# Fourier stage of a two-layer trunk: half the channel columns, time folded a second time, mirrored channels joined in the output weights

## The reference, cut to what matters

```python
def fourier_mix(u, w_f):
    B, T, _ = u.shape
    ug = u.astype(F32).reshape(B, T, FNET_GROUPS, FNET_GROUP_DIM)
    f = jnp.fft.fftn(ug, axes=(1, 3), norm="ortho").real.astype(u.dtype).reshape(B, T, FNET_WIDTH)
    return f @ w_f
```

## Time and profile before

| | |
|---|---|
| median of 3 runs | 2941.22 us (2939.51 to 2941.58) |
| span of the profiled execution | 2938.6 us |
| busy: TensorE, its weight loads | 2877.4 us, 2756.4 us |
| busy: VectorE, ScalarE, GpSimd | 1330.6, 1076.5, 614.0 us |
| instructions | 44082, of which 18396 matmul passes |
| granted clock of TensorE | 0.996 of full speed over the span |

### The profile page before, as it was taken

How to read it: one execution, slowest core, us unless ns; L and a number is a source line. 1 busy time by engine, 2 the same in 40 slices (tenths; PEclk the granted TensorE clock), 3 DMA queues, 4 the chain that set the end, 5 groups by cost and what they waited for, 6 DMA issues and landing times.

```text
span 2938.6 us, 44082 instructions
## 1 busy us (share of the span) xinstructions
PE 2877.4 (98%) x18396; PEld 2756.4 (94%) x18396; DVE 1330.6 (45%) x2291; ACT 1076.5 (37%) x1947; POOL 614.0 (21%) x312
## 2 busy tenths in 40 slices
PE   6999999999999999999999999999999999999998
PEld 5999999999999999999999999999999989899997
DVE  4343443123557575446344434421146567554543
ACT  4333333221444544422343333323133444443231
POOL 0221221122221212122431221211221121211242
PEclk9999999999999999999999999999999999999999
DMA  5332224102111102254421121220211111215532
GB/s 224 102 110 82 102 90 137 67 15 78 42 47 47 48 32 94 80 203 141 133 79 65 66 82 39 94 83 22 70 41 45 44 48 47 78 51 183 165 110 94
DMA packets 84278, 248.55 MB, mean 85 GB/s; under 512 B 9201, under 2 KB 30193, under 8 KB 83057
## 3 DMA queue, kind: packets, MB, share of 16 engines
q1 hardware_dynamic: 84080, 245.74, 24.5%
HBM read 191.71 MB, written 54.00 MB: 84 GB/s over the span
## 4 chain that ended last, share of the span: by engine, by line
PE 89%; DVE 5%; ACT 2%; DMA 2%; issue 1%; SPq 1%; DVEq 0%; POOL 0%; POOLq 0%; ACTq 0%
PE ps L730 44%; PE ps L713 18%; PE ps L823 6%; PE ps L769 6%; PE ps L900 3%; PE ps L1041 3%; PE ps L1032 2%; PE ps L961 2%; PE ps L888 2%; PE ps L943 1%; DVE e L1839 1%; DVE stat L1822 1%; ACT e L1435 1%; DMA wmod<-w_mod 1%; DVE aTl L1846 1%
## 5 line engine op out<-in xcount | busy, mean ns | idle before, releaser
L730 PE MATMUL ps<-hhi,whi 128*128 128x384 f32 x2640 | 916.3, 347 | 5.7 <-DVE obuf L1854 3.3
L730 PE MATMUL ps<-hhi,wlo 128*128 128x384 f32 x2640 | 886.3, 336 | 0.0
L730 PE MATMUL ps<-hlo,whi 128*128 128x384 f32 x2640 | 884.1, 335 | 0.0
L1956 POOL TENSOR_TENSOR wlo<-wraw,whi 128x1024 fp32r<-128x1024 f32 (+1 forms) x188 | 415.8, 2212 | 2063.6 <-ACT whi L1127 2063.5
L730 PEld LDWEIGHTS ps<-hhi,whi 128*128 128x128 f32 x2640 | 500.0, 189 | 24.1 <-issue 7.3
L730 PEld LDWEIGHTS ps<-hlo,whi 128*128 128x128 f32 x2640 | 497.1, 188 | 0.9
L730 PEld LDWEIGHTS ps<-hhi,wlo 128*128 128x128 f32 x2640 | 495.9, 188 | 0.0
L1127 ACT ACTIVATE whi<-wraw 128x1024 fp32r<-128x1024 f32 (+1 forms) x188 | 174.5, 928 | 229.9 <-PE ps L713 209.3
L1444 ACT ACTIVATE aTh<-ps 128x512 fp32r<-128x512 f32 (+1 forms) x200 | 96.5, 482 | 278.4 <-PE ps L1032 278.4
L1691 DVE TENSOR_TENSOR ptl<-ps,pth 128x512 fp32r<-128x512 f32 (+1 forms) x144 | 82.1, 611 | 246.8 <-ACT pth L1301 246.6
L1822 DVE TENSOR_REDUCE stat<-ps 128x1 f32<-128x1152 f32 x144 | 176.5, 1231 | 16.9 <-PE ps L769 16.0
(11 more groups left out here) (199 smaller groups left out, 4835.8 us busy)
## 6 DMA issues: line engine op xcount, KB each, us to landing
wraw<-w_in SPq DMA_DIRECT2D x128, 512.0 KB, 4.2
gates_dram<-gst SPq DMA_DIRECT2D x48, 576.0 KB, 3.0
gth<-gates_dram SPq DMA_DIRECT2D x48, 576.0 KB, 4.9
mraw<-w_mod SPq DMA_DIRECT2D x32, 512.0 KB, 3.8
wraw<-w_branch SPq DMA_DIRECT2D x48, 256.0 KB, 2.8
bias<-rpb SPq DMA_DIRECT2D x8, 1280.0 KB, 6.0
outs_dram<-obuf SPq DMA_DIRECT2D x16, 576.0 KB, 3.9
oraw<-outs_dram SPq DMA_DIRECT2D x16, 576.0 KB, 3.8
```

Source lines behind the costliest of these rows:

```text
L730: x = mm(ps[:, bank, 0:CH], a[:, s % 2, k, :], b[:, k, n * CH:(n + 1) * CH], start=(k == 0 and a is whi and b is hhi), stop=(k == KT - 1 a ...
L1956: g_.tensor_tensor(lo[:, 0:kt, :], wraw[:, n % 2, 0:kt, :], hi[:, 0:kt, :].bitcast(F32), ALU.subtract).then_inc(S.w_lo, 1)
```

## The change

The channel DFT takes 65 cosine and 63 sine columns (`COS` = 65), because the others mirror them; the output stands for mirrored channels by two products, and so the rows of `fnet_w` come in twice (`mirrored_rows`), and VectorE joins them (`joined`) in `wraw` before ScalarE splits them. Time is folded twice: `forward` writes each half of the tokens in rising order up to its quarter and in falling order beyond it, `pair` takes four tiles of 128 tokens with 128 columns each, VectorE folds the halves (`xpm`) and then rising with falling (`xst`). The tokens 0 and 512, which have no partner, go through a two-column matmul into `first_t`, and come back as a bias. `over_tokens` has 8 matmuls in two banks instead of 16 in four; the cosine and sine rows stand in one stationary operand, and where mirrored frequencies are written into `ft`, the sine rows change sign (`signs`).

```diff
+COS = P // 2 + 1
+UH = TL // 2 + 1
...
-    tab_t = [raw(f"tab_t{j}", [P, 4, HK + 2]) for j in range(3)]
-    tab_c = raw("tab_c", [P, 2, P])
+    tab_t = [raw(f"tab_t{j}", [P, 4, HK + 2]) for j in range(2)]
+    tab_c = raw("tab_c", [P, P])
+    tab_x = raw("tab_x", [P, 2, P])
...
-                    sp.dma_start(wraw[:, n % 2, 0:chunk_k(c), :], weight(*c)).then_inc(w_load[n % 2], 16)
+                    kt = KT if c[0] == "w" else chunk_k(c)
+                    sp.dma_start(wraw[:, n % 2, 0:kt, :], weight(*c)).then_inc(w_load[n % 2], 16)
...
+            for out, src in ((craw[:], cvec), (gcol[:], norm_g), (bcol[:], b_mod), (subg[:], subln_g), (fgcol[:], final_g),
+                             (signs[:], fsigns)):
...
-                        pe.wait_ge(S.tab_load, 96 * (l + 1))
+                        pe.wait_ge(S.tab_load, 64 * (l + 1))
                         pe.wait_ge(*evacuated("u", l, "fn", g))
-                    if j < 2 and g:
-                        pe.wait_ge(*((S.q_done, 2 * n), (S.f_ctx, n))[j])
-                    if j >= 2:
-                        pe.wait_ge(S.folded, n * 5 + j - 1)
-                    for i, t in enumerate((j, j + 4) if j < 4 else (8,)):
-                        x = mm(ps[:, 6 + j % 2, 256 * i:256 * i + 256], uT[:, g % 2, t * P:(t + 1) * P],
-                               tab_c[:].rearrange("p a b -> p (a b)"), start=True, stop=True)
+                    if j == 1 and g:
+                        pe.wait_ge(S.f_ctx, n)
+                    if j == 2:
+                        pe.wait_ge(S.folded, n * 3 + 1)
+                        mm(ps[:, 6, 0:P], uT[:, g % 2, 2 * UH:], tab_c[:], start=True, stop=True)
+                        mm(ps[:, 6, P:P + 2], tab_c[:], uT[:, g % 2, 0:2 * UH:UH], start=True, stop=True
+                           ).then_inc(S.u_pair, 1)
+                        return
+                    up, down = 1 + P * j, TL // 4 + 1 + P * j
+                    for i, at in enumerate((up, down, UH + up, UH + down)):
+                        x = mm(ps[:, 6 + j, i * P:(i + 1) * P], uT[:, g % 2, at:at + P], tab_c[:], start=True, stop=True)
                     x.then_inc(S.u_pair, 1)
 
                 def over_channels(g):
 
-                    return {j + 2: (lambda j=j: pair(g, j),) for j in range(5)}
+                    return {j + 2: (lambda j=j: pair(g, j),) for j in range(3)}
+
+                def tokens_free(g):
+
+                    pe.wait_ge(S.q_done, 2 * (l * HEADS + g))
+                    pe.wait_ge(S.f_ctx, l * HEADS + g)
 
                 def over_tokens(g):
 
                     n = l * HEADS + g
-                    pe.wait_ge(S.folded, n * 5 + 4)
-                    for i, bank in enumerate((3, 4, 5, 6)):
-                        if bank == 6:
-                            pe.wait_ge(S.folded, n * 5 + 5)
-                        x_in, part = ((xsum, 0), (xsum, 1), (xdif, 0), (xdif, 1))[i]
-                        width = (HK + 1) if i < 2 else HK
-                        for j in range(4):
-                            x = mm(ps[:, bank, 0:width], x_in[:, j, part, :], tab_t[j][:, i, 0:width],
-                                   start=(j == 0), stop=(j == 3))
+                    pe.wait_ge(S.folded, n * 3 + 3)
+                    for odd in range(2):
+                        width = HK if odd else HK + 1
+                        for j in range(2):
+                            for part in range(2):
+                                x = mm(ps[:, 3 + odd, 0:width], xst[:, j, odd, part, :], tab_t[j][:, 2 * odd + part, 0:width],
+                                       start=(j == 0 and part == 0), stop=(j == 1 and part == 1))
                         x.then_inc(S.x_done, 1)
...
-                pe.wait_ge(S.q_done, 2 * (l * HEADS + 1))
+                tokens_free(1)
...
+                    if SPLIT[s][0] == "w":
+                        act.wait_ge(S.w_joined, SPLIT[s][1] * HEADS + SPLIT[s][3] + 1)
...
-                    grid = uT[:, g % 2, 0:TL].rearrange("p (r c) -> p c r", c=GW)
+                    both = uT[:, g % 2, 0:2 * UH].rearrange("p (h t) -> p h t", t=UH)
+                    up = both[:, :, 0:TL // 4].rearrange("p h (r c) -> p c h r", c=GW)
+                    down = both[:, :, TL // 2:TL // 4:-1].rearrange("p h (r c) -> p c h r", c=GW)
                     for i, (a, b) in enumerate(((0, 24), (24, 48), (48, GW))):
-                        fn(grid[:, a:b], u_in[:, i, 0:(b - a) * GH].rearrange("p (c r) -> p c r", r=GH), ACT.Copy)
-                    fn(uT[:, g % 2, TL:], u_in[:, 2, TL - 2 * CH:], ACT.Copy).then_inc(S.act_evac, 1)
+                        src = u_in[:, i, 0:(b - a) * GH].rearrange("p (c h s r) -> p c h s r", h=2, s=2, r=4)
+                        fn(up[:, a:b], src[:, :, :, 0], ACT.Copy)
+                        fn(down[:, a:b], src[:, :, :, 1], ACT.Copy)
+                    fn(both[:, :, TL // 4], u_in[:, 0, 4:GH:8], ACT.Copy)
+                    fn(uT[:, g % 2, 2 * UH:], u_in[:, 2, TL - 2 * CH:], ACT.Copy).then_inc(S.act_evac, 1)
 
                 def pair_copies(g, under):
 
                     split_to(SPLIT_NO[under] + 2)
-                    for j in range(4):
-                        act.wait_ge(S.u_pair, 5 * (l * HEADS + g) + j + 1)
-                        fn(xcs[j % 2][:].rearrange("p a b -> p (a b)"), ps[:, 6 + j % 2, 0:256], ACT.Copy
-                           ).then_inc(S.pair_copied, 1)
+                    for j in range(2):
+                        act.wait_ge(S.u_pair, 3 * (l * HEADS + g) + j + 1)
+                        fn(xab[j][:], ps[:, 6 + j, 0:2 * P], ACT.Copy).then_inc(S.pair_copied, 1)
 
                 def over_tokens(g):
 
                     n = l * HEADS + g
-                    for i in range(2):
-                        act.wait_ge(S.x_done, 5 * n + 2 * i + 2)
-                        w = (HK + 1) if i == 0 else HK
-                        if g:
-                            act.wait_ge(S.q_done, 2 * (n - 1) + i + 1)
-                        fn(qsb[:, i, 0:w], ps[:, 4 if i == 0 else 6, 0:w], ACT.Copy).then_inc(S.q_copied, 1)
-                    act.wait_ge(S.x_done, 5 * n + 5)
                     if g:
                         act.wait_ge(S.f_lo, n)
+                    act.wait_ge(S.x_done, 3 * n + 1)
+                    fn(ft[:, 0:TL // 2 + 1:2], ps[:, 3, 0:HK + 1], ACT.Identity, bias=first_t[:, 2:3]).then_inc(S.q_even, 1)
+                    act.wait_ge(S.q_done, 2 * n + 1)
+                    fn(ft[:, 1:TL // 2:2], ps[:, 4, 0:HK], ACT.Identity, bias=first_t[:, 3:4])
+                    act.wait_ge(S.x_done, 3 * n + 3)
                     fn(ft[:, TL:], ps[:, 7, 0:P], ACT.Copy).then_inc(S.f_ctx, 1)
...
-                    for j in range(4):
-                        dve.wait_ge(S.pair_copied, 4 * n + j + 1)
-                        hi = ps[:, 6 + j % 2, 256:512]
-                        lo = xcs[j % 2][:].rearrange("p a b -> p (a b)")
-                        v.tensor_tensor(xsum[:, j].rearrange("p a b -> p (a b)"), lo, hi, ALU.add)
-                        v.tensor_tensor(xdif[:, j].rearrange("p a b -> p (a b)"), lo, hi, ALU.subtract
-                                        ).then_inc(S.folded, 1)
-                    dve.wait_ge(S.u_pair, 5 * n + 5)
-                    v.tensor_copy(xctx[:].rearrange("p a b -> p (a b)"), ps[:, 6, 0:256]).then_inc(S.folded, 1)
+                    for j in range(2):
+                        dve.wait_ge(S.pair_copied, 2 * n + j + 1)
+                        if g == 0 and j == 0:
+                            v.memset(xst[:, :, :, 0, COS:], 0.0)
+                            v.memset(xst[:, :, :, 1, 0:COS], 0.0)
+                            v.memset(xctx[:, 0, COS:], 0.0)
+                            v.memset(xctx[:, 1, 0:COS], 0.0)
+                        if g and j == 0:
+                            dve.wait_ge(S.x_done, 3 * n)
+                        v.tensor_tensor(xpm[:, j, 0], xab[j][:], ps[:, 6 + j, 2 * P:], ALU.add)
+                        v.tensor_tensor(xpm[:, j, 1], xab[j][:], ps[:, 6 + j, 2 * P:], ALU.subtract)
+                        dve.drain()
+                        for odd in range(2):
+                            x, y = xpm[:, j, odd, 0:P], xpm[:, j, odd, P:]
+                            v.tensor_tensor(xst[:, j, odd, 0, 0:COS], x[:, 0:COS], y[:, 0:COS], ALU.subtract if odd else ALU.add)
+                            z = v.tensor_tensor(xst[:, j, odd, 1, COS:], x[:, COS:], y[:, COS:], ALU.add if odd else ALU.subtract)
+                        z.then_inc(S.folded, 1)
+                    dve.wait_ge(S.u_pair, 3 * n + 3)
+                    if g:
+                        dve.wait_ge(S.f_ctx, n)
+                    v.tensor_copy(xctx[:, 0, 0:COS], ps[:, 6, 0:COS])
+                    v.tensor_copy(xctx[:, 1, COS:], ps[:, 6, COS:P])
+                    v.tensor_scalar(first_t[:, 0:2], ps[:, 6, P:P + 2], signs[:, 2:3], None, ALU.mult)
+                    dve.drain()
```

(63 more changed lines are left out.)

29 lines of the change are left out of this document (12 added, 17 removed).

## The result

The changed kernel takes 2916.69 us (median of four executions), the kernel before 2940.63 in the same comparison: ratio 0.9917, 95% interval 0.9903 to 0.9931. One of the four took 7128.71 us and is a slow one; the other three lie between 2915.36 and 2916.96, and the ratio goes by them alone. The changed kernel is faster by 23.9 us where 37.4 were forecast, and its time lies 2.7 us above the range. The profiled spans differ by 24.0 us, from 2938.6 to 2914.6.

The account below looks back on a forecast made before the run. TensorE, busy 98% of the span, was taken as the bound: 2941.2 less 40.8 (5.10 us in each of eight groups), plus 2.9 for the first groups' gaps and 0.5 for the start, gives 2903.8 us; range 2900.5 to 2914.

Parts of the forecast that it names:

- Tokens, -3.46 a group: TensorE's token matmuls: 16 passes for 32 at the same widths, 3.46 us less a group.
- Channels, -1.64: TensorE's channel matmuls: narrower passes, with two-column ones at 0.20 us, take 2.23 us for 3.87 a group.
- Rival 1, the runs of four: ScalarE's scattered copies priced by the run: `forward` 5.0 us for 2.1, u3 and z0 late, 2913.6 us; chance 0.14.
- Rival 2, weight loads: Operand loads don't fit under 128-column passes: 144 passes cost 0.035 us more each, about 2909 us; chance 0.12.
- Rival 3: Slower than before: `forward` eats all the gain, near 9.6 us; at 12 us the kernel takes 2955; chance 0.01.
- Groups 1 to 3, `pair(g, 2)` on `folded`: Third pair's wait on VectorE stays covered: copy 0.4 us, folds 1.5, against 4.0 us of TensorE work.
- a new wait that had not been seen: Unforeseen wait that leaves less than half of the gain; chance 0.03.
- The gap is 2.5 for 1.1: TensorE's wait before the first group's third pair: 1.45 us more in each layer, 2.9 in all.
- The start, +0.5: One more small load on SP's chain at the start: 0.5 us more, between 0 and 0.5.
- Output weights, "slack over 4 us": Doubled load and VectorE's join ahead of the split stay covered; tightest is w3, with over 4 us slack.
- Stages that the change does not touch, priced at 0: Context matmuls, projections and output jobs keep their count and size: 0.

Follow-up runs that it names:

- h_all: Changed kernel with the edits of a_port and c_chain, and the sign table's load issued after the first weights; 2897.92 us, ratio 0.9856.
- a_port: Changed kernel, but GpSimd makes a group's low part only when VectorE has folded both tiles of the next group; 2908.49 us, ratio 0.9890.
- c_chain: b_memset, and ScalarE copies the pairs of group 0 before it splits the next weights; 2902.30 us, ratio 0.9873.
- e_pad: Kernel before with two unused 32-byte tiles, so that everything behind them lies 64 bytes further on; 2941.80 us, ratio 1.0005.
- i_scale: h_all with the two mul_a instructions for the next layer moved ahead of the branch sum's last low part on VectorE; 2893.53 us, ratio 0.9839.
- b_memset: Changed kernel with the four memsets of group 0 ahead of the wait for the first pair copy; 2914.21 us, ratio 0.9912.

## Why the prediction was wrong

The direction was right, and so was the price of TensorE's own passes. The size was off by 13.5 us, because waits that the prediction held to be covered were not, and because a pause was priced at its length. By the prediction's own steps:

- **Tokens, -3.46 a group: right.** 3.46 for 16 passes. **Channels, -1.64: right but for the third pair.** Eight passes take 0.90; `pair(g, 2)` takes 0.34 (0.22 for L946 and, in h_all, 0.12 for L947), so the groups of two columns cost the 0.12 of L785 and not 0.20. Behind a wait it takes 0.61.
- **Rival 1, the runs of four: out.** The copies of 192 columns have a mean of 530 and 549 ns, `forward` takes 2.1 us, and u3 and z0 find their banks. **Rival 2, weight loads: out.** 0.90 for eight, not 1.2. **Rival 3** falls with rival 1.

```profile
L1354 ACT ACTIVATE uT<-ps 128x192 f32<-128x192 f32 x16 | 8.8, 549 | 0.0
L1353 ACT ACTIVATE uT<-ps 128x192 f32<-128x192 f32 x16 | 8.5, 530 | 77.4 <-PE ps L717 77.4
```

- **"Groups 1 to 3, `pair(g, 2)` on `folded`: copy 0.4, two folds and four small ones 1.5, against 4.0 us" is the step that failed.** It summed VectorE's own durations and forgot that VectorE is not alone. The old folds read one operand out of PSUM; the new small folds read two out of SBUF, and one of them falls on GpSimd's `flo` in all six groups, 0.04 to 0.08 us behind its start. The fold is 2.7 us longer, and the slack was 2.1: 6 x 0.65 us of waits and 6 x 0.27 in the pair behind, 5.5 us. a_port shows it. The chances gave 0.03 to a new wait that had not been seen.
- **"The gap is 2.5 for 1.1": nearly right as a gap (2.88 and 2.71), wrong as a price.** The sum took a pause at its own length. The clock fell behind it, a term that stood at nothing. It cost 1.5 us in layer 0 and 2.6 in layer 1 on the 99 passes, and 0.4 on the third pair of layer 1 (0.80 and 0.22 us for 0.49 and 0.12). c_chain shows it. In the gap itself `forward` took 2.1 us as before and not 0.3 more, the memsets took 0.7 and not 0.5, and the first small fold 0.58 for 0.22, beside GpSimd's `wlo`.
- **The start, +0.5: the load was right, the start was not.** 0.6 for the shift of tiles and some 2.1 for the clock were not in the sum; here +3.3 in all.
- **Output weights, "slack over 4 us": right.** The 288 passes behind them take 50.25 us for 50.30 before, without a wait.
- **Stages that the change does not touch, priced at 0: wrong in both directions.** For it, the shift: 2.1 to 2.9 us in layer 1 (e_pad: 2.8). Against it, other pairs of VectorE and GpSimd whose meeting is a matter of when they come. The output stage waits 3.9 us for 1.6 (+2.3) and loses 1.3 more to the clock; i_scale shows both. As e_pad has that wait too, neither this loss nor the shift's gain can be put to the Fourier stage. In the attention stages of the changed kernel the waits on VectorE are longer by 1.0 and 1.9 us; one row stands for it, the product L1882, with two SBUF inputs, whose shortest, median and longest durations in layer 1 are

```profile
L1882 DVE SCALAR_TENSOR_TENSOR e<-e,stat,e x36: 352/1418/3492, 2157.8 to 2632.2; 128x1152 f32<-128x1152 f32 x32, 128x128 f32<-128x128 f32 x4
```

where h_all has 1420 as the longest. The long one begins at 2327.81, 0.12 us behind the start of a `wlo` of GpSimd that takes 2.39 us, so it looks like the same thing; no run moved it.

The 13.4 us between forecast and profile, summed: start +2.8; gaps +0.5 and the clock behind them +4.5; port +5.5; attention stages +2.9; output stage +2.3 and its clock +1.3; shift -5.6 (twice e_pad's 2.8, which was read in layer 1). That is 14.2; the 0.8 over is less than the 2.7 us by which one row differed between two executions of the kernel before. Only the port and the gaps with their clock, 10.5 us together, are shown by runs to come from the change. What was missed is of two kinds: one engine's instruction made long by another, and a pause that costs more than itself. The range was too narrow because its bounds came from the prices of passes and copies and from the one bare chain, and none from what another engine does beside them.

## What to carry to other kernels

Before an operation of VectorE is counted as covered, look at where its operands lie and what GpSimd does in that moment: with both in SBUF it may last as long as GpSimd's instruction (here 2.93 us for 0.21). So either keep one operand in PSUM, or move one of the two by an ordering that costs nothing. A pause of TensorE that grows from 1.1 to 2.7 us is to be priced with the slower passes behind it. The cure here was the order on another engine: ScalarE's two small copies ahead of the big split, with the memsets early, were worth 14 us, of which some 10 are the pauses and their clock and 3.5 fell elsewhere, in the output stage. Before an instruction is taken out of a chain, see what the next one will then meet: in b_memset it was the same port. When stages that an edit doesn't touch change by a per mille, profile the old kernel twice and add unused tiles of the same size to it before looking for a reason in the edit.

## What the hardware showed

- 8 or 63 columns on VectorE with both inputs in SBUF take 2.37 and 2.93 us when GpSimd (2.47 and 2.90 us an instruction) has begun just before; alone they take 0.15 (0.23 for the two, which overlap) and 0.21.
- Pauses of TensorE of 0.94 and 1.1 us left the granted clock at 1.00, and so did six of the seven between 1.62 and 1.71 us; behind the seventh (1.68 us, c_chain, at 2317.8) it was 0.66 over the next 5 us. A pause of 2.44 us in the output stage stands in all twelve traces: in ten the next 5 us had 0.66 to 0.70, in two 1.00. Behind all eight of 2.71 to 2.94 us before the third pair and all seven of 3.9 us it was 0.50 to 0.70. So the length of a pause alone doesn't decide. In the changed kernel 1.3 to 3.0 us were lost behind one.
- Scattered copies of ScalarE cost the same in runs of 4 as in runs of 16: 530 to 549 ns for 192 columns, where 0.25 us and 1.6 ns a column gives 557.
- Unused tiles that shift others by 64 bytes made long runs of matmuls 0.7% faster (140.46 us for 141.50) and the first load 3% slower (20.34 us for 19.72). Why is open, and the time of the whole kernel didn't change clearly (2941.80 us for 2939.55).
